# Spreading the softmax reciprocals of the first mixer by transfers over main memory instead of transposes and a copy

## What is computed

```
p = h @ fox_w_in                              # queries, keys, values, gates, memory queries
q, k = rmsnorm(q) * 64 ** -0.5, rmsnorm(k)
logits = q @ k.T + cum[..., None] - cum[:, :, None, :]     # 12 heads, causal
p = softmax(logits, axis=-1)                  # exponents divided by their row totals
o_mix = p @ v
o_mem = softmax(rmsnorm(qm) @ rmsnorm(k_mem).T) @ v_mem    # 4 heads, 256 keys
x = x + concatenate([o_mix, o_mem], axis=-1) @ w_out
x = x + conv_ffn(rmsnorm(x))
```

## Time and profile before

| | |
|---|---|
| Median of three runs | 2064.19 us (2063.45 to 2066.13) |
| The profiled execution, device time | 2063.42 us |
| Its span, first to last instruction | 2061.6 us |
| TensorE (PE) busy | 2044.8 us, 99% |
| VectorE (DVE) busy | 1283.7 us, 62% |
| ScalarE (ACT) busy | 967.5 us, 47% |
| GpSimd (POOL) busy | 39.2 us, 2% |
| Share of PE in the chain that ended last | 97% |
| Read from main memory, written to it | 181.47 MB, 2.10 MB |

### The profile page before, as it was taken

One profiled execution on the slowest core, in us unless ns is written; L12 is line 12 of the kernel. 1 busy time (PEld: TensorE's weight loads), 2 busy tenths in 40 slices (PEclk: granted clock), 3 DMA queues, 4 the chain that ended last, 5 costly groups with the idle time before them and its releaser, 6 DMA issues.

```text
span 2061.6 us, 29301 instructions
## 1 busy us (share of the span) xinstructions
PE 2044.8 (99%) x10730; PEld 1719.4 (83%) x10730; DVE 1283.7 (62%) x2128; ACT 967.5 (47%) x1907; POOL 39.2 (2%) x86
## 2 busy tenths in 40 slices
PE   8999999999999999999999999999999999999999
PEld 8998888888889788888888888888889878888887
DVE  8556688557756987774677455344548995534542
ACT  7666574334447865542344343233345764322331
POOL 0000001000000000000000000000001000000000
PEclk9999999999999999999999999999999999999999
DMA  6212233333333112333333333333332123333332
GB/s 222 67 39 70 76 91 100 97 97 97 97 90 102 31 42 62 96 99 97 97 96 95 99 96 97 97 97 98 94 96 77 32 83 97 98 97 97 97 100 86
DMA packets 103535, 185.48 MB, mean 90 GB/s; under 512 B 11744, under 2 KB 21344, under 8 KB 103136
## 3 DMA queue, kind: packets, MB, share of 16 engines
q1 hardware_dynamic: 103392, 183.61, 30.6%
HBM read 181.47 MB, written 2.10 MB: 89 GB/s over the span
## 4 chain that ended last, share of the span: by engine, by line
PE 97%; ACT 2%; DVE 1%; issue 0%; DMA 0%; POOL 0%; POOLq 0%; DVEq 0%; ACTq 0%
PE PSA L2032 26%; PE PSA L2034 26%; PE PSA L2033 26%; PE PSA L2050 3%; PE PSA L2052 3%; PE PSA L2051 3%; PE PSA L2138 2%; PE PSA L2164 2%; PE PSA L2150 2%; PE PSA L2092 1%; ACT PP L2563 1%; PE PSA L2121 0%; PE PSA L2174 0%; PE PSA L2131 0%; PE PSA L2065 0%
## 5 line engine op out<-in xcount | busy, mean ns | idle before, releaser
L2493 ACT ACTIVATE WH<-RAW 128x512 fp32r<-128x512 f32 (+2 forms) x669 | 415.6, 624 | 802.9 <-PE PSA L2034 679.3
L2207 DVE TENSOR_TENSOR WL<-RAW,WH 128x512 fp32r<-128x512 f32 (+2 forms) x669 | 454.4, 682 | 372.1 <-ACT WH L2493 350.3
L2032 PE MATMUL PSA<-HNh,WH 128*128 128x512 f32 x1440 | 562.5, 391 | 0.0
L2034 PE MATMUL PSA<-HNh,WL 128*128 128x512 f32 x1440 | 560.3, 389 | 0.0
L2033 PE MATMUL PSA<-HNl,WH 128*128 128x512 f32 x1440 | 560.2, 389 | 0.0
L2033 PEld LDWEIGHTS PSA<-HNl,WH 128*128 128x128 f32 x1440 | 270.3, 188 | 57.1 <-issue 1.2
L2032 PEld LDWEIGHTS PSA<-HNh,WH 128*128 128x128 f32 x1440 | 270.3, 188 | 57.0 <-issue 1.2
L2034 PEld LDWEIGHTS PSA<-HNh,WL 128*128 128x128 f32 x1440 | 270.3, 188 | 56.3
L2032 PE MATMUL PSA<-Gh,WH 128*128 128x512 f32 x704 | 273.9, 389 | 0.0
L2033 PE MATMUL PSA<-Gl,WH 128*128 128x512 f32 x704 | 273.9, 389 | 0.0
L2034 PE MATMUL PSA<-Gh,WL 128*128 128x512 f32 x704 | 273.9, 389 | 0.0
(11 more groups left out here) (305 smaller groups left out, 2417.7 us busy)
## 6 DMA issues: line engine op xcount, KB each, us to landing
RAW<-in_w SPq DMA_DIRECT2D x623, 256.0 KB, 2.6
RAW<-in_w SPq DMA_DIRECT2D x54, 192.0 KB, 2.5
XT<-in_x SPq DMA_DIRECT2D x8, 256.0 KB, 5.1
MT<-in_mem SPq DMA_DIRECT2D x2, 1024.0 KB, 4.8
out_x<-XT SPq DMA_DIRECT2D x8, 256.0 KB, 2.1
RAW<-in_w SPq DMA_DIRECT2D x8, 208.0 KB, 2.4
RAW<-in_w SPq DMA_DIRECT2D x8, 134.0 KB, 4.5
PAR<-in_par SPq DMA_DIRECT2D x1, 207.0 KB, 3.3
```

The lines of the kernel that those rows point to most:

```text
L2032: pe.matmul(out, wh, xh, start=(a["start"] and c == 0), stop=False)
L2034: p = pe.matmul(out, wl, xh, start=False, stop=ends)
L2207: dve.tensor_tensor(l, r, h, ALU.subtract).then_inc(done.sem("split.dve"), 1)
L2493: act.activation(h, r, ACT.Copy).then_inc(done.sem("split.act"), 1)
```

## The change

Only the eight jobs of the first mixer are changed. The steps `pwide`, `pbcast` and `pspread` are no longer made. In their place SyncE issues four DMAs for each job: two (`pspill`) write the reciprocals of the two heads from SBUF, 4 bytes at a time, as rows of 512 numbers into a buffer in main memory (two such buffers, used in turn); once both have landed, two more (`pfetch`) read each row back 64 times, into 64 partitions of F. They stand in SyncE's list right behind `precip`, and `pmul` waits for `pfetch`. The step `pmul` is put into the list right after the last `pvals`, where before it came a round later, behind `pbcast` and `pspread`. A `PSTAT` buffer is free for the job after the next once `pspill` has landed, no longer once `pwide` is done.

```diff
@@ Pairs.score
-                    pstats.take(jkey, [("pwide.pool", jkey)])
+                    pstats.take(jkey, [("pspill.dma" if self.by_dma else "pwide.pool", jkey)])
@@ Pairs.recip
                 step("precip", jkey, job=job, S=S, last=self.end(n))
+                if self.by_dma:
+                    after(0.4, lambda: self.spread_by_dma(n, S))
+                    return
                 i = tmp.take(("inv", jkey), [("pbcast.pe", jkey)])
                 step("pwide", jkey, S=S, inv=TMP[i], before=tmp.before["inv", jkey])
+
+            def spread_by_dma(self, n, S):
+
+                jkey, ckey, at = (self.id, n), (self.id, self.jobs[n].chunk), len(spills)
+                spills.append(jkey)
+                x = tmp.take(("pmix", ckey), [("pmix.dve", ckey)])
+                older = [("pfetch.dma", spills[at - 2])] if at > 1 else []
+                step("pspill", jkey, S=S, rows=SHARE[at % 2], before=older)
+                done.mark("pspill.dma", jkey)
+                step("pfetch", jkey, rows=SHARE[at % 2], F=TMP[x], at=at, before=tmp.before["pmix", ckey])
+                done.mark("pfetch.dma", jkey, f"pfetch{at % 2}.dma")
...
@@ Pairs.older (and the same in run_by_twos)
-                cost = self.sums(*turned) if ends and not late else 0
+                cost = self.sums(*turned) if ends and not late and not self.by_dma else 0
                 cost += self.values(*turned) if turned else 0
+                if ends and self.by_dma:
+                    after(0.4, lambda: self.mix(turned[0]))
@@ the first mixer's jobs
-        att = Pairs(jobs, fox_free, [VMEM[:, 1, :, :].rearrange("p a b -> p (a b)"), RS[1][:, :]])
+        att = Pairs(jobs, fox_free, [VMEM[:, 1, :, :].rearrange("p a b -> p (a b)"), RS[1][:, :]], True)
@@ sync
+                elif k == "pspill":
+                    for t in a["before"]:
+                        w.wait_ge(*done(*t))
+                    w.wait_ge(*done("precip.dve", key))
+                    for x in range(2):
+                        sp.dma_start(a["rows"][x, :].rearrange("(i t) -> t i", i=4), a["S"][:, x, 3, :],
+                                     allow_slow_non_contiguous=True).then_inc(done.sem("pspill.dma"), 16)
+                elif k == "pfetch":
+                    for t in a["before"]:
+                        w.wait_ge(*done(*t))
+                    w.wait_ge(*done("pspill.dma", key))
+                    for x in range(2):
+                        r = slice(64 * x, 64 * x + 64)
+                        sp.dma_start(a["F"][r, :], a["rows"][x:x + 1, :].broadcast_to([64, T])).then_inc(
+                            done.sem("pfetch%d.dma" % (a["at"] % 2)), 16)
```

More of the change, by code:

```diff
@@ L284, in memset, with dma_start @@
         return self.took(0.1 + size_of(out) / 960)
-    def dma_start(self, out, a):
+    def dma_start(self, out, a, allow_slow_non_contiguous=False):
         return self.took(max(0.47, size_of(out) / 586))
@@ L544 @@
     "pmix": ("pmix.dve",),
+    "pspill": (),
+    "pfetch": (),
     "memload": (),
@@ L1024, in scaled @@
                 step("scale", g, norm=self, bank=b)
-        n_att = [0]
+        n_att, spills = [0], []
+        SHARE = [nc.dram_tensor(f"share{i}", (2, T), F32, kind="Internal").ap() for i in range(2)]
         class Pair:
@@ L1095, in program, with __init__ @@
         class Pairs:
-            def __init__(self, jobs, free, extra=None):
-                self.jobs, self.free, self.at = jobs, free, {}
+            def __init__(self, jobs, free, extra=None, by_dma=False):
+                self.jobs, self.free, self.at, self.by_dma = jobs, free, {}, by_dma
                 self.PT = [x[:, :] for x in PT] + (extra or [])
@@ L1199, in recip @@
                 step("precip", jkey, job=job, S=S, last=self.end(n))
+                if self.by_dma:
+                    after(0.4, lambda: self.spread_by_dma(n, S))
+                    return
                 i = tmp.take(("inv", jkey), [("pbcast.pe", jkey)])
                 step("pwide", jkey, S=S, inv=TMP[i], before=tmp.before["inv", jkey])
+            def spread_by_dma(self, n, S):
[7 more added lines that the diff above has]
+                done.mark("pfetch.dma", jkey, f"pfetch{at % 2}.dma")
+                for name, by in (("pspill.dma", 32), ("pfetch.dma", 32)):
+                    sem, count = done.value[name, jkey]
+                    done.value[name, jkey] = (sem, by * count)
+                need([("pspill.dma", jkey)])
             def mix(self, n):
@@ L1207, in mix @@
                 F, h, l = TMP[tmp.of["pmix", key]], AOH[:, job.chunk, :], AOL[:, job.chunk, :]
-                step("pmul", key, last=self.end(n), F=F, h=h, free=free)
+                step("pmul", key, last=self.end(n), F=F, h=h, free=free,
+                     spread=("pfetch.dma", (self.id, n)) if self.by_dma else ("pspread.act", key))
                 after(1.2, lambda: step("pmix", key, F=F, h=h, l=l))
@@ L1231, in run_by_twos @@
                         if self.jobs[turned[0]].sealed(turned[1][-1]):
-                            ended = turned[0]
+                            if self.by_dma:
+                                after(0.4, lambda n=turned[0]: self.mix(n))
+                            else:
+                                ended = turned[0]
                     if tile:
@@ L2352, in vector @@
                     w.wait_ge(*done("pvals.pe", a["last"]))
-                    w.wait_ge(*done("pspread.act", key))
+                    w.wait_ge(*done(*a["spread"]))
                     dve.tensor_tensor(F, PS[6][:, :], F, ALU.mult).then_inc(done.sem("pmix.mul"), 1)
```

## The result

The changed kernel takes 2108.16 us (2107.30 to 2108.58, four runs) beside 2063.82 us for the kernel before (2063.14 to 2066.13, four runs): a ratio of 1.0212, with a 95% interval of 1.0200 to 1.0225. The prediction was 2062.0, between 2059.0 and 2072.0. That was wrong: the kernel lost 44.3 us.

The account below looks back on a forecast made before the run. PE, busy 99% of the span, was taken to bound the kernel. Removed transposes -3.4 us and waiting +1.2 gave -2.2 on the profiled 2063.4, so 2061.2, and a median of 2062.0, range 2059.0 to 2072.0.

Parts of the forecast that it names:

- What is removed: On PE, 32 transposes go, 0.43 us for each of 8 jobs, shortening the end by 3.4 us.
- The spill's landing: Reciprocals written to main memory: landing taken as 3.5 us, between 2.0 and 7.0, within 7.2 us from reciprocal to F.
- the estimate of 0.7 us: Spill priced by the skill page's small packets, 64 per engine, on top of a landing; 0.8 us below the prediction's sum.
- The fetch's landing: Reading the rows back into F: landing taken as a weight load's 2.6 us, between 2.2 and 4.1.
- I count half of DVE's standing as PE's: DVE stands 0.3 us at each pmul; half reaches PE, 8 x 0.15 = 1.2 us.
- the spare times of the prediction: How long PE's transposes start after their exponents are ready: 0.05 to 7.0 us over 44 steps, median 1.7.
- F is late: Rival: 4-byte pieces land late, DVE stands at pmul; 2076.8 us with F at 10; slower by over 0.2%: 0.23.
- That isn't the measure: At pmul, not the earlier 12.7 us gap but the planner's place for F counts, 6.9 us after the reciprocal.
- The last job: Before the projection, F's way stays hidden with 2.6 us to spare; F after 12.2 us would cost 2.4.
- The loads behind the spills: In SyncE's queue, weight loads behind job 5's spill go about 3.5 us later, hidden by 16 us of cover.
- the signs of being wrong: Spills landing after 5 us or more, pmul waiting over a microsecond, or ACT waiting for SyncE's loads.
- Bank 6 is freed sooner than before: In PSUM, bank 6 frees earlier and one bank less is taken; both can only help, no size given.

Follow-up runs that it names:

- no_spill: The changed kernel without its spills, the fetch reading weight rows instead, no division by row totals; 2060.59 us against 2065.22 for the kernel before.
- spill_16b: The changed kernel with each partition's four reciprocals written as one 16-byte piece, F read in steps; 2060.71 us against 2065.22 for the kernel before.
- own_lines: The changed kernel with 4-byte pieces written 64 bytes apart, the fetch reading weights instead; 2060.88 us against 2065.22 for the kernel before.
- late_unplanned: no_spill with the pair of fetches made three times in a row, the planner seeing one pair; 2103.61 us against 2063.66 for the kernel before.
- own_rows: The changed kernel with one partition's four pieces 8 bytes apart in its own 64 bytes, fetch from weights; 2065.32 us against 2065.69 for the kernel before.
- apart_8b: The changed kernel with 4-byte pieces written 8 bytes apart, the fetch reading weights instead; 2068.40 us against 2065.69 for the kernel before.
- late_fetch: no_spill with the pair of fetches made three times in a row, the planner seeing all three; 2062.38 us against 2064.49 for the kernel before.
- planned: The changed kernel with only the planner's cost of a spill raised from 0.47 to 4.2 us; 2071.38 us against 2065.22 for the kernel before.
- two_blocks: spill_16b with the last block's six attention jobs spreading reciprocals the same way; 2068.38 us against 2064.49 for the kernel before the change.
- two_blocks_plain: two_blocks with F read without steps in the last block, so its quotients are mixed up; 2064.27 us against 2063.66 for the kernel before the change.

## Why the prediction was wrong

1. **What is removed: right.** I counted 3.4 us for 32 transposes. `no_spill` and `spill_16b` gained 4.6 and 4.5 us, with intervals of 2.3 to 6.0 and 2.1 to 5.8 that hold the 3.4.
2. **The spill's landing: the step that failed.** "I take 3.5 [...] with ends 2.0 and 7.0". It was about 10 (9.2 to 10.8 in the chain), outside both ends. I bounded it by the number of pieces and the bytes in each, and the number was harmless (2.5 us in `own_lines`). Where the pieces land was never asked: eight fell into each 32 bytes. The form stood in the diff, a distance of 512 bytes between one partition's pieces and of 4 bytes between neighbouring partitions'. No row of before has such a write, so the upper end should have been open. The Trainium skill's rule that I weighed ("DMA: Bandwidth & Descriptors", section "Rules for kernel authors": one descriptor per element when the last dimension is strided) named the right line of the diff, and the trace agrees with it: packets under 512 B rise from 11744 to 20448, by 8192 pieces and 512 more. Its figure of 10.5 ns per small packet, with the estimate of 0.7 us from it, is near what `own_lines` shows (a landing of 2.5 us against 2.0 in `spill_16b`), and misses the 10.7 of the dense form.
3. **The fetch's landing: right.** 2.6 foreseen, 2.9 measured.
4. **"I count half of DVE's standing as PE's": the second step that failed.** DVE stood for 49.1 us, and the loss to `no_spill` is 48.9; in `late_unplanned` it is 43.0 and 44.6. For these long waits the factor is about 1.0, not 0.5: most of them are 5 to 9 us, and the spare times of the prediction had a median of 1.7. For short waits the half is not refuted: `own_rows` and `apart_8b`, with 11.2 and 10.0 us in waits of at most 2.5, are 4.3 and 7.3 us behind `no_spill`, each by its own kernel before, a factor of 0.4 and 0.7 from one run each. The clock adds to what PE stands: 34.0 us idle, and about 0.07 x 234 = 16 us (an estimate) for a mean granted clock of 0.93, give 50. I had no term for the clock. So my rival "F is late" was the right one, but priced too low: it took F at 10 us, 3.1 us after its planned place, as 16 us of loss. With the factor of 1.0 that is 8 x 3.1 = 25 us, or 2085.6 instead of 2076.8.
5. **"That isn't the measure", the planned place is: right, and stronger than I used it.** The prediction said that DVE keeps the planned order and that the planner counts on 6.9 us. It did not go on to say that nearly all time beyond 6.9 falls on DVE, job after job: 6.1 us a job, where F came 7.1 to 8.0 us behind its place in five of the eight. And it did not ask what F costs when the order allows for it: in `late_fetch`, F at 10 to 12 us costs 2.5 us over `no_spill`.
6. **The last job: right in kind, not in size.** The chain shows `pmul`, high and low part bare before chunk 5, and PE waits 2.2 us for them, as it does in `planned`. But F came after 14.9 us, and the prediction's 2.4 belong to 12.2; by its working 14.9 would cost 2.4 + 2.7 = 5.1. That only 2.2 are seen is luck of the order: the last `pvals` now comes at 270.83, 4.9 us after the reciprocal's end at 265.96, where it was 2.8 before (227.23 to 229.99), so PE had more to do meanwhile.

```profile
266.46 10.50 DMA share<-PSTAT
...
277.53 3.33 DMA TMP<-share
...
280.95 0.70 DVE TMP L2381
...
281.68 0.64 ACT AOH L2602
...
282.34 0.70 DVE AOL L2384
...
283.08 0.50 PE PSA L2059
```

7. **The loads behind the spills: not hidden, but no main cause.** SyncE is held for 76 us in all, about 9.5 a job and not 4. One of ACT's splits waits 5.3 us for a load that went only at 116.00, behind the fetch of job 1; this was one of the signs of being wrong. The low part of the same weights, for which PE waits 5.4 us, stood behind a `pmul` that waited until 118.56 in any case, and came 0.4 us after it. `planned` has the same held queue at +6.2 us.
8. **"Bank 6 is freed sooner than before": wrong.** The late `pmul` holds it longer, and one `pvals` waits 4.7 us for it (4.6 in `planned`).

## What to carry to other kernels

Before values are written to main memory for a transfer to spread, look at where neighbouring pieces land: put pieces of 4 bytes 32 bytes or more apart, or write each partition's values as one piece and take the other order at the reader, as `spill_16b` does (0.9981 of the kernel before, the best version here). If the reader is the engine that bounds the stage, its stepped reads can cost more than they save (3.3 us in the last block, against 2.6 expected from the transposes). Where an order is planned ahead, a wrong latency costs far more than a long one: an F as late cost 2.5 us with an order made for it and 44.6 without, over `no_spill`; so measure the landing and give it to the planner before judging such a change.

## What was not expected of the hardware

- The landing of 4-byte writes depends on how many fall into the same 32 bytes: from issue to fetch 3.4 us for one, 4.4 for two, 5.2 to 5.5 for four, 10.7 for eight. For four it makes no difference whether they are of one partition or of several. The DMA engines are nearly idle in that time (0.02 busy for 9 us).
- A float32 multiplication or subtraction of 128x512 on DVE that reads with a step of 16 bytes takes 1.08 to 1.09 us (`two_blocks`); the same without a step takes 0.68 (`two_blocks_plain`).
- Waits of some microseconds on PE, job after job, brought the mean granted clock from 1.00 to 0.93 over 234 us, by estimate a third of the loss.
